# Sums over partitions for head norms and rotary norms, as float32 products or as pairs of rounded products

## The reference

```python
o = hgrn2_scan(...)                                       # first block, 8 heads of 128
o = rms_norm(o, hg_norm_w) * jax.nn.silu(hg.reshape(B, T, HG_HEADS, HG_DV))

q = axial_rope(rmsnorm(heads_first(qa, A_HEADS, HEAD_DIM), q_g), ang_row, ang_col)     # second block
k = axial_rope(rmsnorm(heads_first(ka, A_KV_HEADS, HEAD_DIM), k_g), ang_row, ang_col)

def rmsnorm(x, g):
    r = lax.rsqrt(jnp.mean(xf * xf, axis=-1, keepdims=True) + NORM_EPS)
    return (xf * r * g).astype(x.dtype)
```

## Time and profile before

| | |
|---|---|
| median of 3 runs | 1892.91 us (1892.76 to 1894.31) |
| the profiled execution | 1891.33 us, of which 1889.5 us are the profile's span |
| TensorE busy | 1874.0 us, 99% |
| VectorE, ScalarE, GpSimd busy | 1101.6, 889.1, 149.8 us |
| float32r products of 256 columns, L445 | the largest groups: 541.5, 530.9, 462.1 us of the first ones listed |
| DMA | 347.75 MB, 184 GB/s on average |
| mean granted TensorE clock | 0.999 of full |

### The profile page before, as it was taken

How to read it: one execution, slowest core, us unless ns; L and a number is a source line. 1 busy time by engine, 2 the same in 40 slices (tenths; PEclk the granted TensorE clock), 3 DMA queues, 4 the chain that set the end, 5 groups by cost and what they waited for, 6 DMA issues and landing times.

```text
span 1889.5 us, 33863 instructions
## 1 busy us (share of the span) xinstructions
PE 1874.0 (99%) x13420; PEld 1739.9 (92%) x13420; DVE 1101.6 (58%) x1270; ACT 889.1 (47%) x1171; POOL 149.8 (8%) x133
## 2 busy tenths in 40 slices
PE   9999999999999999999999999999999999999998
PEld 9989998999999889988998899899889999899986
DVE  6655766567655555555445544554565556767664
ACT  6534444455544445443444344344454345674543
POOL 1001322411001100000010000001010000000000
PEclk9999999999999999999999999999999999999999
DMA  8656555566565656656665665566556665354454
GB/s 274 192 179 172 183 179 177 166 198 182 166 232 191 215 183 179 196 197 192 196 192 193 193 193 192 193 194 190 189 180 179 178 180 155 111 164 146 156 191 143
DMA packets 176915, 347.75 MB, mean 184 GB/s; under 512 B 11152, under 2 KB 11360, under 8 KB 176256
## 3 DMA queue, kind: packets, MB, share of 16 engines
q1 hardware_dynamic: 174176, 337.76, 57.2%
q0 software_dynamic: 2608, 8.08, 1.7%
HBM read 342.37 MB, written 2.10 MB: 182 GB/s over the span
## 4 chain that ended last, share of the span: by engine, by line
PE 96%; DVE 2%; ACT 1%; issue 0%; DMA 0%; SPq 0%; DVEq 0%; ACTq 0%
PE ps L445 58%; PE ps L457 33%; PE ps L547 1%; DVE wlo L1288 1%; PE ps L770 1%; PE ps L737 1%; PE ps L760 1%; ACT whi L886 0%; PE ps L780 0%; DMA raw<-in_w_in_dram 0%; PE ps L475 0%; PE ps L748 0%; PE ps L598 0%; PE ps L590 0%; DVE xlo L1310 0%
## 5 line engine op out<-in xcount | busy, mean ns | idle before, releaser
L1288 DVE TENSOR_TENSOR wlo<-raw,whi 128x1024 fp32r<-128x1024 f32 x631 | 796.7, 1269 | 694.2 <-ACT whi L886 693.2
L886 ACT ACTIVATE whi<-raw 128x1024 fp32r<-128x1024 f32 x631 | 664.3, 1058 | 882.7 <-PE ps L445 552.5
L445 PE MATMUL ps<-xhi,whi 128*128 128x256 f32 (+1 forms) x1904 | 541.5, 284 | 0.2 <-DVE wlo L1288 0.2
L445 PE MATMUL ps<-xhi,wlo 128*128 128x256 f32 (+1 forms) x1904 | 530.9, 279 | 0.0
L445 PE MATMUL ps<-xlo,whi 128*128 128x256 f32 x1664 | 462.1, 278 | 0.0
L445 PEld LDWEIGHTS ps<-xhi,whi 128*128 128x128 f32 x1904 | 359.2, 189 | 8.4 <-issue 6.5
L445 PEld LDWEIGHTS ps<-xhi,wlo 128*128 128x128 f32 x1904 | 357.8, 188 | 0.0
L445 PEld LDWEIGHTS ps<-xlo,whi 128*128 128x128 f32 x1664 | 313.0, 188 | 1.3 <-issue 0.5
L445 PE MATMUL ps<-x2hi,whi 128*128 128x256 f32 x1024 | 282.8, 276 | 0.0
L445 PE MATMUL ps<-x2lo,whi 128*128 128x256 f32 x1024 | 282.7, 276 | 0.0
L445 PE MATMUL ps<-x2hi,wlo 128*128 128x256 f32 x1024 | 282.7, 276 | 0.0
(11 more groups left out here) (371 smaller groups left out, 2368.5 us busy)
## 6 DMA issues: line engine op xcount, KB each, us to landing
raw<-in_w_in_dram SPq DMA_DIRECT2D x279, 512.0 KB, 3.8
raw<-in_w_up_dram SPq DMA_DIRECT2D x128, 512.0 KB, 3.7
raw<-in_w_down_dram SPq DMA_DIRECT2D x128, 512.0 KB, 3.6
raw<-in_w_out_dram SPq DMA_DIRECT2D x64, 512.0 KB, 4.0
raw<-in_w_branch_a_dram SPq DMA_DIRECT2D x16, 512.0 KB, 4.7
raw<-in_w_branch_b_dram SPq DMA_DIRECT2D x16, 512.0 KB, 4.0
x_nat<-in_x_dram SPq DMA_DIRECT2D x4, 512.0 KB, 7.0
rel<-in_rel_turned_dram POOLq DMA_DIRECT2D x8, 256.0 KB, 4.3
```

The costliest lines, as they stand in the source:

```text
L445: ins = mm(outs[b], w[:, k % SLOTS, j, cols], v, start=start, stop=last and j == CK - 1 and i == 2, skip_group_check=True)
L886: f(whi[:, k % SLOTS], raw[:, k % SLOTS], ACT.Copy).then_inc(whi_ready, 1)
L1288: tt(wlo[:, k % SLOTS], raw[:, k % SLOTS], whi[:, k % SLOTS], ALU.subtract).then_inc(wlo_ready, 1)
```

## The change

The squares are split like the weights: ScalarE rounds them to float32r (high part), VectorE subtracts the high part from the square (low part, rounded as well), and TensorE multiplies ones in float32r with both parts, adding the second product to the first in PSUM. A float32 product becomes two float32r products. For the head norms the parts go to `ya_hi` and `ya_lo`, which are free until group 17; `hg_upper` therefore waits for the sums. `hg_squares` moves from behind chunk 7 of group 14 to behind chunk 1 of group 15, the logarithms to iteration 2, the exponentials to iterations 3 to 6, and the three transposes to behind chunk 4. The high parts are made in iterations 4 to 7 of group 14, the low parts in iterations 5, 6, 7 of group 14 and 0 of group 15, each behind VectorE's split of that iteration. For the rotary sums the high part stands in ScalarE's `evac_in2` between squaring and scaling; the low part is on VectorE, at the place before the sum, behind split and side work. The places of the rotary sums stay.

```diff
+        ones_r = sb("ones_r", [P, P], F32R)
...
+        qs_hi = at("qs_hi", 80, [P, 4, TM], F32R)
+        qs_lo = at("qs_lo", 84.25, [P, 4, TM], F32R)
...
             def hg_squares():
 
+                pe.wait_ge(ones_ready, 1)
                 pe.wait_ge(hg_os, 4)
-                pe.wait_ge(hg_o2, 4)
+                pe.wait_ge(hg_o2h, 4)
+                pe.wait_ge(hg_o2l, 4)
                 for i in range(4):
-                    ins = mm(misc[:, i, :], ones[:], o2_hg[:, 2 * i:2 * i + 2, :], start=True, stop=True)
+                    for n, v in enumerate((ya_hi, ya_lo)):
+                        ins = mm(misc[:, i, :], ones_r[:], v[:, 2 * i:2 * i + 2, :], start=n == 0, stop=n == 1)
                 ins.then_inc(hg_ss, 1)
...
-                    if k == 7 and g == G_HGOUT:
+                    if k == 1 and g == G_HGOUT + 1:
                         hg_squares()
-                    if k == 2 and g == G_HGOUT + 1:
+                    if k == 4 and g == G_HGOUT + 1:
                         pe.wait_ge(hg_sd, 4)
                         shift_phase(4, lambda i: acc[:, i, :])
...
             def rope_squares(n, s):
 
-                pe.wait_ge(nr_ev, 2 * n + 1)
+                pe.wait_ge(nr_hi, n + 1)
+                pe.wait_ge(nr_lo, n + 1)
...
-                    src = qsq[:, i, :] if n == 0 else qsq[:, 2 * i:2 * i + 2, 0:T]
                     w = TM if n == 0 else 2 * T
-                    ins = mm(ps[:, 2 * s + i, 0:w], ones[:], src, start=True, stop=True)
+                    for m, v in enumerate((qs_hi, qs_lo)):
+                        src = v[:, i, :] if n == 0 else v[:, 2 * i:2 * i + 2, 0:T]
+                        ins = mm(ps[:, 2 * s + i, 0:w], ones_r[:], src, start=m == 0, stop=m == 1)
...
+            def hg_squares_upper(i):
+
+                act.wait_ge(hg_o2, i + 1)
+                f(ya_hi[:, 2 * i:2 * i + 2, :], o2_hg[:, 2 * i:2 * i + 2, :], ACT.Copy).then_inc(hg_o2h, 1)
...
+                    if g == G_HGOUT and 4 <= k <= 7:
+                        hg_squares_upper(k - 4)
-                    if g == G_HGOUT + 1 and k == 0:
+                    if g == G_HGOUT + 1 and k == 2:
                         for i in range(4):
                             hg_root(i)
-                    if g == G_HGOUT + 1 and k % 2 == 0:
-                        hg_inverse(k // 2)
+                    if g == G_HGOUT + 1 and 3 <= k <= 6:
+                        hg_inverse(k - 3)
...
                     f(qsq[:, :, 0:T], qg[:, :, 0:T], ACT.Square).then_inc(nr_ev, 1)
                     act.wait_ge(nr_ev, 2 * n + 1)
+                    f(qs_hi[:, :, 0:T], qsq[:, :, 0:T], ACT.Copy).then_inc(nr_hi, 1)
                     f(qg[:, :, 0:T], qg[:, :, 0:T], ACT.Copy, scale=gvec[:, 1:2]).then_inc(nr_ev, 1)
...
+            nc.vector.tensor_copy(ones_r[:], ones[:]).then_inc(ones_ready, 1)
...
+            def hg_squares_lower(i):
+
+                dve.wait_ge(hg_o2h, i + 1)
+                tt(ya_lo[:, 2 * i:2 * i + 2, :], o2_hg[:, 2 * i:2 * i + 2, :], ya_hi[:, 2 * i:2 * i + 2, :],
+                   ALU.subtract).then_inc(hg_o2l, 1)
...
+                    if g == G_HGOUT and 5 <= k <= 7:
+                        hg_squares_lower(k - 5)
+                    if g == G_HGOUT + 1 and k == 0:
+                        hg_squares_lower(3)
...
+            def rope_squares_lower(n):
+
+                nb, w = (2, TM) if n == 0 else (4, T)
+                dve.wait_ge(nr_hi, n + 1)
+                if n:
+                    dve.wait_ge(nr_ss, n)
+                tt(qs_lo[:, 0:nb, 0:w], qsq[:, 0:nb, 0:w], qs_hi[:, 0:nb, 0:w], ALU.subtract).then_inc(nr_lo, 1)
...
                     if j >= J_B:
                         side(NC * (j - J_B) + k)
+                    if NC * j + k + 1 in ROPE_FROM:
+                        rope_squares_lower(ROPE_FROM.index(NC * j + k + 1))
```

More of the change, by code:

```diff
@@ L280, in program @@
         hg_s, hg_m, hg_acc, hg_q, hg_k, hg_g = [sem(n) for n in ("hg_s", "hg_m", "hg_acc", "hg_q", "hg_k", "hg_g")]
-        hg_o, hg_os, hg_o2, hg_ss, hg_sd, hg_rs, hg_t, hg_y, hg_hi, ya_ready = [sem(n) for n in (
-            "hg_o", "hg_os", "hg_o2", "hg_ss", "hg_sd", "hg_rs", "hg_t", "hg_y", "hg_hi", "ya_ready")]
+        hg_o, hg_os, hg_o2, hg_o2h, hg_o2l, hg_ss, hg_sd, hg_rs, hg_t, hg_y, hg_hi, ya_ready = [sem(n) for n in (
+            "hg_o", "hg_os", "hg_o2", "hg_o2h", "hg_o2l", "hg_ss", "hg_sd", "hg_rs", "hg_t", "hg_y", "hg_hi", "ya_ready")]
         at_s, at_nm, at_exp, at_p, at_t, at_pt, at_pv, at_hi, at_y = [sem(n) for n in (
@@ L287, in program @@
         vt_t, vt_c = [sem("vt_t0"), sem("vt_t1")], [sem("vt_c0"), sem("vt_c1")]
+        ones_ready, nr_hi, nr_lo = [sem(n) for n in ("ones_ready", "nr_hi", "nr_lo")]
         nr_ev, nr_ss, nr_sd, nr_rs, nr_swap, nr_done = [sem(n) for n in (
@@ L1007, in hg_upper @@
                 act.wait_ge(hg_y, i + 1)
+                act.wait_ge(hg_ss, 1)
                 f(ya_hi[:, 2 * i:2 * i + 2, :], o_hg[:, 2 * i:2 * i + 2, :], ACT.Copy).then_inc(hg_hi, 1)
@@ L1135, in evac_in2 @@
                     act.wait_ge(nr_ev, 1)
+                    f(qs_hi[:, 0:2, :], qsq[:, 0:2, :], ACT.Copy).then_inc(nr_hi, 1)
                     f(qg[:, 0:2, :], qg[:, 0:2, :], ACT.Copy, scale=gvec[:, 2:3]).then_inc(nr_ev, 1)
```

## The result

The changed kernel takes **1917.27 us** (median of 4 runs, 1916.18 to 1920.71). The kernel before took 1893.06 us in the runs beside it (median of 4, 1892.76 to 1894.31). The ratio is 1.0131, with a 95% interval from 1.0119 to 1.0143: slower by 24.2 us. The forecast was 1915.8 in a range from 1907 to 1921. The profiled execution took 1916.64 us, with a span of 1913.9.

What follows compares the result with a forecast made beforehand. TensorE was taken to bound the kernel. Head norms +2.1, rope sums +2.7, +5.2 and +7.5, and two clock falls +5.4 made +22.9 us, hence 1915.8 us, range 1907 to 1921.

Steps and rivals of the forecast that it cites:

- TensorE is the bound, and each wait is paid: Whole kernel: time is saved only where TensorE gets less work; every microsecond it waits is paid in full.
- The reading that no wait was longer than 1.5 us: Profile before the change: TensorE's longest wait was read as 1.5 us.
- The four waits: Head norms' sum and rope sums 0 to 2: TensorE waits 4.2, 3.1, 6.2 and 8.3 us for VectorE's subtractions.
- The turns of VectorE and GpSimd: Head norms: VectorE and GpSimd's gate products alternate by whole instructions, delaying the fourth subtraction to 376.2, a 4.2 us wait.
- Rival C: Head norms: GpSimd's gate products don't hold up VectorE, wait only 0.6 us; 1912.2 us in all, chance 0.06.
- The saving of the products: All four sums: rounded products start 0.23 us apart instead of 0.43, saving TensorE 3.6 us.
- the pace behind them: Projection products behind the head norms' sums: slower pace may not set in after a rounded product, 0.5 us gained.
- rival D: All four sums: rounded products with ones run at the old rate, 3.6 us more, 1919.4 us; chance 0.03.
- The clock: Rope sums 1 and 2: TensorE falls to half clock after each wait, 2.7 us lost per fall, 5.4 in all.
- rival B: Head norms: the clock falls after that wait too; 1918.5 us in all, chance 0.13.
- Rival E: All four sums: VectorE subtracts ahead of its other work, waits eat the saving, no clock fall; 1892.7 us, chance 0.05.
- Rival F: All four sums: TensorE finds every lower part ready; 1888.8 us, faster, chance 0.03.

Runs made afterwards that it cites:

- order: Changed kernel with VectorE's three rope subtractions moved ahead of its split, side work and norm halves: 1904.95 us.
- hg_pool: hg_only with GpSimd's two gate products held back until VectorE has made all four head-norm subtractions: 1892.70 us.
- late2: Changed kernel with head norms' sums two chunks later, rope sums one place later, ScalarE's rope squares and roundings and VectorE's rope subtractions re-placed: 1887.79 us.
- late2_f32: late2 without rounding and subtraction, its sums in float32 on the unsplit squares: 1892.52 us.
- again_rope: rope_only once more, unedited, with one profiled run: 1912.23 us.
- fill: Changed kernel with 35, 25, 53 and 72 unread transposes on TensorE ahead of the four waits: 1911.32 us.
- hg_only: Kernel before with only the head norms' half of the change, rope sums left in float32: 1896.55 us.
- late: Changed kernel with head norms' sums two chunks later, rope sums one or two places later, ScalarE's scaling, subtractions and square roots postponed: 1899.20 us.
- rope_only: Kernel before with only the rope sums' half of the change, head norms' sums unchanged in place and format: 1913.71 us.

## Why the prediction was right, and where it was not

**TensorE is the bound, and each wait is paid.** Right. Behind the first 0.5 us the lag grows at the four places and nowhere else, and 24.3 us of it stand at the end. The reading that no wait was longer than 1.5 us overlooked the 3.0 us at the kernel's start, which both kernels have, so nothing hangs on it.

**The four waits.** Worked out as 4.2, 3.1, 6.2 and 8.3 us; measured as 4.17, 3.24, 6.25 and 8.44. Each came from following VectorE's queue in the order of the code, with durations from rows of before. Running order and hg_pool shows that the queue is the cause: a change in that order or in GpSimd's alone takes the waits away where it was expected to, rope sum 2 excepted.

**The turns of VectorE and GpSimd.** Right. The prediction's list for the head norms had the fourth subtraction done at 376.2; the trace has it start at 375.64 and last 0.68. Rival C is refuted by hg_pool.

**The saving of the products** (3.6 us, and 0.5 for the pace behind them). 0.23 us per product is right, rival D out. In the traces of late2 and late2_f32 the products themselves save 3.4 us. Between the medians it is 4.7, with a spread of some 3.5 us in each kernel's runs. The 0.5 us for the pace had a wrong reason. The prediction tied the slow pace to the float32 sum, but in again_rope the fast pace was back four chunks behind a float32 sum, and in hg_pool a rounded one was followed by the slow pace. In fill the lag does fall by 0.8 us over the chunks behind the head norms' sum, against a kernel before that had the slow pace in its profiled execution. That the term came out near its size is luck of the executions. At the head norms fill lags by 1.5 us where the prediction had 2.1. The pace explains half of that difference, and the rest wasn't taken apart.

**The clock is the term that was wrong in its parts.** The step said: falls after the waits of 6.2 and 8.3 us, 4.2 on the edge, 3.1 not, 2.7 us each, 5.4 in all. There were four falls in the profiled execution, of 1.7, 1.7, 2.4 and 1.8 us of lost time by the windows, 7.6 in all, or 6.0 between the medians with and without them. The wait of 4.2 us brought a fall in each of the four profiles that hold it (the changed kernel's two, hg_only, order), and that of 3.24 in three of four. So the step failed in "4.2 is on the edge, 3.1 is not", and late shows a fall behind 2.0 us. The price per fall had come from the start of the kernel, where half speed was put at some 5.4 us of work from the distances of the transposes; the granted clock is listed as 1.00 there. Behind the short waits it was 3.4 us, and behind the long ones part of it passed while TensorE was still waiting. Twice as many falls at about half the price nearly cancelled, so the total held: 5.4 us forecast, 6.0 measured. That is luck, not understanding. By its number of falls the case was neither the forecast nor rival B but one step beyond B. The rule quoted from the Trainium skill (TensorE: Matmul & The Clock Gate, "HAM oscillation") held: waits between matmuls did bring the half rate back. That the same wait may or may not do so is shown by the two executions of rope_only.

**Rival E** had its mechanism right and its place wrong. With VectorE's order turned, rope sums 0 and 1 wait less than 1 us. But for rope sum 2 the time of 1685.7 supposed a subtraction ahead of the previous step's split and norm half too, and took no account of ScalarE, whose own split of that step stands behind the rounding and the scaling. Its 0.7 us at rope sum 0 were counted from 1553.87, though the earlier trace rows have TensorE there at 1554.33; from there it is 0.3.

**Rival F**, every lower part ready, gave 1888.8. late2 brings that about and measures 1887.8. What the change lacked for it was one or two places of distance, not speed. That late failed and late2 didn't shows that the distance has to be found on three queues at once, ScalarE's above all.

## What to carry to other kernels

When TensorE is the bound, a cheaper matmul that needs one more elementwise step is worth its saving only if that step is done before TensorE asks. Follow the queue of the engine that does it, instruction by instruction, with everything ahead of it there, table loads and the other engine's turns included. Price a new wait at its length and add the half-clock work behind it, 1.2 to 2.2 us for each of the four waits here. Don't count on a short wait to keep the clock: 3.24 us did once and failed three times, and 2.0 us failed in late. Before giving the idea up, move producer and consumer apart by a place or two, and look at what the move pushes back in turn.

## What the runs showed of the hardware that was not expected

- The fall of the clock isn't decided by the program alone. Behind a wait of 3.24 us the granted clock stayed full in one execution of rope_only and fell to 0.50 for 3.4 us in another, which cost that one 1.6 us on the spot. In the changed kernel the stretches at 0.50 were 3.4, 3.4, 6.8 and 6.8 us once and 6.8, 3.4, 6.8 and 10.2 us another time, with the same waits. This is part of the spread of its runs (1916.2 to 1920.7). The shortest wait with a fall behind it was 2.0 us, in late; each of the twelve profiles also has a wait of 1.5 to 1.7 us in the second block, at the product with `pt`, and none has a fall behind it.
- At full clock the projection products around the head norms start 0.113 us apart in some chunks and 0.118 in others. Behind the head norms' sum 70 of them fall in 8 us in rope_only and 73 in again_rope, the same kernel. The form of the sum doesn't decide it: hg_pool has 71 behind the rounded one. Its cause is open, and it makes a difference of 1 us between executions at this place alone.
- Filling a wait with transposes that nobody reads gave 6.0 us back, although TensorE's useful work starts no earlier.
